# Third block's input linear by seven products of half size, with weight sums on GpSimd and rope angles in later slots

## The reference

```python
def third_block(x, c, positions, ...):
    h = rms_norm(x, g_pre) * (1 + scale) + shift
    proj = h @ w_in
    (q_lat, kv_lat, k_rope, z_mla, q_mb, k_mb, v_mb, z_mb, merge_logits) = split_cols(proj)
    q = rms_norm(q_lat, g_q_lat) @ w_uq             # with a rope part
    kv = rms_norm(kv_lat, g_kv_lat) @ w_ukv         # keys and values
    o_mla = causal_dense_attention(rope(q), [k, rope(k_rope)], v)
    y_mla = (o_mla * silu(z_mla)) @ w_o_mla
    o_mb = moba_attention(rope(q_mb), rope(k_mb), v_mb)
    y_mb = (o_mb * silu(z_mb)) @ w_o_moba
    g_a, g_b = split(sigmoid(merge_logits + b_merge))
    y = (g_a * y_mla + g_b * y_mb) @ w_out
    return x + gate * rms_norm(y, g_post)
```

## Time and profile before

| | us |
|---|---|
| median of three runs | 2348.59 |
| lowest, highest | 2347.05, 2350.40 |
| span of the profiled execution | 2347.6 |
| PE busy in it | 2237.0 (95%) |
| block 3, by PE's timeline | about 2080 to the end |

### The profile page before, as it was taken

One profiled execution on the slowest core, in us unless ns is written; L12 is line 12 of the kernel. 1 busy time (PEld: TensorE's weight loads), 2 busy tenths in 40 slices (PEclk: granted clock), 3 DMA queues, 4 the chain that ended last, 5 costly groups with the idle time before them and its releaser, 6 DMA issues. The chain is left out here.

```text
span 2347.6 us, 35478 instructions
## 1 busy us (share of the span) xinstructions
PE 2237.0 (95%) x14663; PEld 1529.2 (65%) x14663; DVE 912.5 (39%) x1950; ACT 421.2 (18%) x905; POOL 433.0 (18%) x363
## 2 busy tenths in 40 slices
PE   8999999999999998998999999999999999999997
PEld 7888899986799987877633333333333333368786
DVE  4242465645444655526323332222222222253322
ACT  2210220024111024124111111111111111123231
POOL 0110598720188850112000000000000000000000
PEclk9999999999999999999999999999999999999999
DMA  6334744465754444300999999999999999953322
GB/s 263 132 117 143 253 162 157 167 229 204 319 182 165 162 177 171 108 20 2 409 407 429 427 427 429 428 429 412 422 427 428 428 429 428 426 220 130 126 75 87
DMA packets 61009, 619.34 MB, mean 264 GB/s; under 512 B 6784, under 2 KB 8064, under 8 KB 12288
## 3 DMA queue, kind: packets, MB, share of 16 engines
q1 hardware_dynamic: 59184, 611.08, 65.0%
q10 hardware_dynamic: 1712, 6.63, 0.8%
HBM read 616.63 MB, written 1.05 MB: 263 GB/s over the span
## 5 line engine op out<-in xcount | busy, mean ns | idle before, releaser
L2966 PE MATMUL ps<-expert_ring,moe_xg 128*64 128x512 f32 x1280 | 282.1, 593 | 10.4 <-DMA expert_ring<-we_dram 10.2
L3005 PE MATMUL ps<-expert_ring,mix_y 128*64 128x512 f32 x1024 | 228.6, 596 | 10.4 <-DMA expert_ring<-we_dram 10.3
L2966 PEld LDWEIGHTS ps<-expert_ring,moe_xg 128*64 128x64 f32 x1280 | 90.4, 137 | 191.0 <-issue 166.9
L461 PE MATMUL ps<-x_res,ring 128*128 128x256 f32 x896 | 201.4, 383 | 8.7 <-DMA x_res<-x_dram 8.7
L461 PEld LDWEIGHTS ps<-x_res,ring 128*128 128x128 f32 x896 | 169.9, 192 | 33.2 <-DMA ring<-w_in_dram 8.6
L3254 DVE TENSOR_SCALAR mix_y<-ps 128x512 f32<-128x512 f32 x32 | 22.1, 691 | 414.8 <-PE ps L2966 414.8
L2785 POOL COPY unscaled_x<-modulations 128x8 f32<-128x8 f32 x1 | 0.2, 197 | 945.6 <-POOLq L3187 945.6
L2966 PE MATMUL ps<-ring,moe_xg 128*64 128x512 f32 x768 | 170.2, 598 | 0.2
L3005 PEld LDWEIGHTS ps<-expert_ring,mix_y 128*64 128x64 f32 x1024 | 69.9, 137 | 146.8 <-issue 127.6
L461 PE MATMUL ps<-third_h,ring 128*128 128x256 f32 x704 | 160.7, 384 | 1.0 <-DVE third_h L3748 1.0
L620 POOL TENSOR_TENSOR seven_weights<-ring 128x512 f32<-128x512 f32 (+1 forms) x72 | 94.1, 1307 | 326.0 <-DVE seven_x_turned L636 289.2
(11 more groups left out here) (607 smaller groups left out, 3365.1 us busy)
## 6 DMA issues: line engine op xcount, KB each, us to landing
expert_ring<-we_dram SPq DMA_DIRECT2D x144, 2048.0 KB, 23.3
ring<-we_dram SPq DMA_DIRECT2D x48, 2048.0 KB, 24.7
ring<-w_in_dram SPq DMA_DIRECT2D x55, 1024.0 KB, 4.9
ring<-ffn_up_dram SPq DMA_DIRECT2D x44, 1024.0 KB, 4.9
ring<-ada_dram SPq DMA_DIRECT2D x36, 1024.0 KB, 4.9
ring<-w_out_dram SPq DMA_DIRECT2D x16, 1024.0 KB, 5.0
ring<-ffn_dn_dram SPq DMA_DIRECT2D x16, 1024.0 KB, 4.9
ring<-ple_g_dram SPq DMA_DIRECT2D x8, 1024.0 KB, 6.1
```

The lines of the kernel that those rows point to most:

```text
L461: mm = pe.matmul(core.ps[:, bank_of[n, c], 0:TOK], w[:, k * PANEL + c * P:k * PANEL + c * P + P], sources[panel](k0 + k), start=(k0 + k == ...
L2966: mm = pe.matmul(ps[out, bank, :], xg[:, j % 4, j // 4, :], w[:, bank * D + at:bank * D + at + 512], start=False, stop=(j == 7))
L3005: mm = pe.matmul(ps[out, 2, :], hidt[:, at_k:at_k + S], w[:, i * D + at:i * D + at + 512], start=False, stop=(k == DT - 1))
```

## The change

Panels 3 to 19 of `w_in3` (17 panels, tiles 6 to 11, 16, 17, 22, 23, 28, 29, 34, 35, 40 to 59) are made by `SevenProducts`, numbered f0 to f16 here. Four things come with it. POOL makes four weight sums for each of them. DVE turns h at slot 0 (`turn_h`). On PE the even slot of such a panel stands behind the fourth of its seven products (`midway`), the odd slot at its end. The angles leave the block ahead of everything at slot 0 and go, a group each, to slots 7 to 10 of DVE; the sines go from slot 7 to 13 of ACT, the first rope from slot 8 to 14, the root of the latents' norm from slot 6 to 5. The copies of the roped key piece go from POOL to ACT, one behind each key tile's evacuation.

```diff
                         if product == 6:
                             mm.then_inc(core.first_done.sem, 1)
+                            if last and seven.midway:
+                                woven.advance()
                     mm.then_inc(core.panel_used.sem, 1)
                     if last:
                         woven.advance()
-                        woven.advance()
+                        if not seven.midway:
+                            woven.advance()
...
-    rope_slot = [8, 16, 16, 17, 17, 22, 22, 23, 23, 40, 41, 42, 43, 46, 47, 49, 50]
+    rope_slot = [14, 16, 16, 17, 17, 22, 22, 23, 23, 40, 41, 42, 43, 46, 47, 49, 50]
...
-        yield 6
+        yield 5
         wait(act, "lat_var", 1)
         act.activation(b3.lat_rs[:, :], b3.lat_rs[:, :], ACT.Sqrt).then_inc(*inc("lat_root"))
-        yield 7
+        yield 13
         wait(act, "angles_done", 1)
...
-        link(dve.tensor_copy(b3.pos[:, :], b3.pos_int[:, :]))
-        rope_angles(dve, link, core, b3)
-        dve.sem_inc(*inc("angles_done"))
         yield 5
         wait(dve, "lat_summed", 1)
...
-        yield 6
         wait(dve, "lat_root", 1)
...
-    def gpsimd(pool):
-
-        wait(pool, "roped", 1)
-        for t in range(DT):
-            pool.wait_ge(core.act_evac.sem, core.act_evac.at(b3.K0[t] + 1))
-            pool.tensor_copy(kv[64:96, t, :], lat[64:96, 3, :]).then_inc(*inc("keyed"))
-        yield
+    def angles(dve):
+        link = core.link("dve", dve)
+        yield 7
+        dve.wait_ge(core.const_loaded.sem, core.const_loaded.at(16))
+        link(dve.tensor_copy(b3.pos[:, :], b3.pos_int[:, :]))
+        for n, slot in enumerate((7, 8, 9, 10)):
+            yield slot
+            rope_angles(dve, link, core, b3, n)
+        dve.sem_inc(*inc("angles_done"))
...
+        def keys(ts):
+
+            def key(t):
+                which, take, _ = plain(kv, (t,))[0]
+
+                def after(e, link, wait_tile):
+                    wait_tile(e, b3.K0[t])
+                    wait(e, "roped", 1)
+                    e.activation(kv[64:96, t, :], lat[64:96, 3, :], ACT.Copy).then_inc(b3.sem["keyed"].sem, 1)
+                return (which, take, after)
+            return [key(t) for t in ts]
...
+        h_turned = s.enter_context(nc.sbuf_tensor("third_h_turned", [P, 4, DT // 2, P], F32))
...
+        seven = SevenProducts(core, s, {"w_in3": (3, turned_h, None, {0: 0})}, core.seven_signals, midway=True, prefix="third_seven_")
+
+        def turn_h(dve):
+            start.at(dve, "h_ready", DT)
+            seven.turn(dve, 0, h[:, 0:4, :], h[:, 4:8, :], *(h_turned[:, i, :, :] for i in (0, 2, 1, 3)))
+            yield
+        linear(core, sources, None, tiles, act_work=positions, banks=3, raw=start, seven=seven,
                weave=Weave((*pe_work, pe_att, outputs, pe_last), (start.shift, act_work, act_att, merge_biases, act_last),
-                           (dve_work, dve_att, dve_last), (pool_work,)))
+                           (turn_h, *dve_work, dve_att, dve_last)))
```

More of the change, by code:

```diff
@@ L563, with __init__ @@
     TURNED = {5: 1, 7: 2, 6: 3, 4: 4}
-    def __init__(self, core, s, parts, signals):
+    def __init__(self, core, s, parts, signals, midway=False, prefix="seven_"):
         def sb(name, shape):
-            return s.enter_context(core.nc.sbuf_tensor("seven_" + name, shape, F32))
-        self.core, self.names, self.groups = core, tuple(parts), {}
+            return s.enter_context(core.nc.sbuf_tensor(prefix + name, shape, F32))
+        self.core, self.names, self.groups, self.midway = core, tuple(parts), {}, midway
         self.first_pair, self.moving_of, self.keepers = {}, {}, {}
@@ L1797, in first_block @@
         parts_fast |= {name: (0, turned_h, keep, groups(name)) for name, keep in (("ffn_dn0", norms[1].keep), ("ffn_dn1", norms[3].keep))}
-        seven = SevenProducts(core, s, parts_fast, [core.counter("seven_" + n) for n in ("summed", "turned", "copied", "combined")])
+        core.seven_signals = [core.counter("seven_" + n) for n in ("summed", "turned", "copied", "combined")]
+        seven = SevenProducts(core, s, parts_fast, core.seven_signals)
         def turn_x(name, first, norm):
@@ L3763, in third_block @@
         b3.Q0, b3.MQ0, b3.MK0, b3.V0, b3.MV0, b3.K0 = 12, 4, 28, 30, 40, (24, 25, 26, 27, 36, 37, 38, 39)
-        pe_work, act_work, dve_work, pool_work, close = projections(core, b3)
+        pe_work, act_work, dve_work, close = projections(core, b3)
         def wait(eng, name, n):
@@ L3789, in third_block, with turned_h @@
                    ("w_om", lambda k: o[:, k, :]), ("w_ob", lambda k: o[:, 4 + k, :]), ("w_out3", lambda k: y[:, k, :])]
-        linear(core, sources, None, tiles, act_work=positions, banks=3, raw=start,
+        h_turned = s.enter_context(nc.sbuf_tensor("third_h_turned", [P, 4, DT // 2, P], F32))
+        def turned_h(product, k0, p):
+            return h_turned[:, {5: 0, 7: 1, 6: 2, 4: 3}[product], p, :]
+        seven = SevenProducts(core, s, {"w_in3": (3, turned_h, None, {0: 0})}, core.seven_signals, midway=True, prefix="third_seven_")
[4 more added lines that the diff above has]
+        linear(core, sources, None, tiles, act_work=positions, banks=3, raw=start, seven=seven,
                weave=Weave((*pe_work, pe_att, outputs, pe_last), (start.shift, act_work, act_att, merge_biases, act_last),
-                           (dve_work, dve_att, dve_last), (pool_work,)))
+                           (turn_h, *dve_work, dve_att, dve_last)))
         close()
```

30 lines of the change are left out of this document (14 added, 16 removed).

## The result

| us | before | after |
|---|---|---|
| median (lowest to highest) of 5 runs each | 2347.82 (2346.72 to 2350.40) | 2392.94 (2388.96 to 2394.91) |
| span of the profiled execution | 2347.6 | 2391.1 |

The changed kernel takes 1.0193 times as long (95% interval 1.0181 to 1.0204), +45.1 by the medians and +43.5 by the two spans. The sign of the forecast holds and its size (+29.6) doesn't: the time lies 2.9 above the range's upper end of 2390. Its main chain was met, and two terms were priced too low.

A forecast was written before the change was run, and what follows sets the result against it. TensorE's own stream, busy 95% of the span, was taken as the bound. Waits (a) to (d) 35.7, with (e) 40.7, less 11.1 saved by seven products, give +29.6, so 2378 us; range 2364 to 2390.

The forecast's parts named there:

- main chain: Fast panels: VectorE and ScalarE begin the even slot's work only after the whole panel is combined, so PE waits.
- the step held to be decisive: Even slot: PE reaches it in mid-panel, 3.57 after the start; VectorE goes on at panel's end +0.67, ScalarE at +0.79.
- (a): Slots 17, 23, 41, 43, 47: PE waits for VectorE's rope steps at a panel's end, 7.1 us in all.
- (b): Slots 35, 45, 47, 51, 53, 57, 59: PE waits for ScalarE's copies and scalings of the even slot, 12.0 us.
- (c): Mid-panel slots 41, 44, 50, 56: PE waits for chains begun only at the panel before's end, 9.2 us.
- (e): Tile 13: two angle groups on VectorE delay the third fast panel's combining; 5.0 us taken, 1.7 uncontended, 7.0 contended.
- What the sums cost: Fast panels: GpSimd's four sums take 5.27 us, below PE's 6.25, so the forecast costed them at nothing.
- the row at 837.00: Earlier trace: after a pause of 2.37 a product took 1.16, 0.1 lost; the forecast's model for waits of 2.
- Rival three: Block 3: the clock falls at each of a dozen waits of about 2 us, 2.0 each, giving 2402; chance 8%.
- (d): First scores, slot 28 to tile 33: PE waits 4.5, next panel 0.5 late, clock drop 2.4; 7.4 us.
- Rivals one and two: One: even slot's work is covered, 2337, 6%. Two: GpSimd's sums set the pace, no change, 2348.5, 4%.

The follow-up runs named there:

- the last versions: Changed kernel with the even slot in mid-panel on all three engines, seven products from panel 6 on, woven slots moved twice; the quoted range has median 2340.04.

## Why the prediction was right and wrong

**Right: the step held to be decisive.** (a) and (b) came out at 7.1 and 12.1 for 7.1 and 12.0, pause by pause. They rest on one chain, panel's end, combining, take, step, whose lengths stand in the earlier trace rows; and the run with the even slot in the middle took them away together with more than half of (c).

**The steps that failed.** The forecast put two things at nothing: what GpSimd's sums do to VectorE's chains, outside the angle groups, and the clock behind every pause but the one at tile 33.

**Right in kind, wrong in reach: contention.** Under (e) the forecast saw that an operation beside a GpSimd sum takes longer, took 5.0 between 1.7 and 7.0, and applied it to the angle groups behind the second panel alone. The trace has it in each place where a VectorE chain meets the sums. The first angle group, which the forecast left out, holds the second panel's combining 1.4 too long for the third. In (c) the ropes ahead of slots 41 and 44 lose 1.4 in two steps (2224.61: 1.38 for 0.42), and one softmax step ahead of 50 and 56 loses 0.8 (2262.69: 1.04 for a step of 128x4). Without the sums (c) is 8.0, so the forecast's 9.2 was 1.2 too much for the chains alone, and the sums add 4.5.

The wait at tile 13, 5.1 for a forecast of 5.0, was met by luck. The two groups that the forecast priced took 7.2 (2124.19 to 2131.4) for its 6.5, since GpSimd had no sums to make in most of that time and waited for weights; the rest came from the first group, at 7.8, which held up what stands behind it. Without the sums tile 13 waits 1.6, and the forecast's end without contention is 1.7. VectorE's and GpSimd's rows there:

```profile
2124.19 1.14 DVE L3516 TENSOR_SCALAR third_tab<-third_pos,mat 128x256 f32<-128x256 f32 x1
...
2131.47 0.29 DVE L650 TENSOR_TENSOR third_seven_second<-third_seven_part,ps 128x128 f32<-128x128 f32 x1
...
2132.11 1.27 POOL L623 TENSOR_TENSOR third_seven_weights<-ring 128x512 f32<-128x512 f32 x1 [6.93 <-DMA ring<-w_in_dram]
```

Under "What the sums cost" the forecast has "I cost it at nothing", and that was the failed sentence. It held for GpSimd's own pace and overlooked its neighbour's. The Trainium skill ("SBUF — State Buffer", section "SBUF: two separate sides") names both kinds of operations, those with two operands in SBUF and those in a two-port mode. The trace agrees for the two-operand kind (the subtractions, 4.20 for 1.34); one-operand steps lose as well (1.24 for 0.29), though no row tells which mode they run in. The forecast used this rule for (e) alone, and it bears on every chain beside the sums.

**Wrong: the clock.** The forecast paid 2.4 for one pause, at tile 33 (trace: 2.8), and nothing for the others, by the row at 837.00. Behind tile 13 it cost 3.1, behind slots 44, 56 and 57 4.8, and filling those pauses and the one at tile 33 gave 8.9 back (6.5 by the stretches). The pauses at 44 and 56 were longer than forecast (3.7 and 3.4 for 2.9 and 2.7), since contention had lengthened them, and so nearer to the one of 3.16 in the earlier trace rows than to those of 2.37. Without the sums, at 2.3 and 2.6, the clock stayed up behind 44 and fell behind 56. Length alone doesn't tell: the pause of 3.2 at slot 50 was followed by matmuls at full pace (2266.87). Rival three had this mechanism at twelve waits of 2.0; the changed kernel's trace shows it at four pauses, and at none of the 1.1 to 2.2 that stand by themselves, but with the pauses filled it came behind 1.90 and 1.76. What decides it beside the pause's length stays open. The 13.9 us between 29.6 and 43.5 are 4.6 in (e), 3.3 in (c), 1.1 in (d) and 4.8 outside the terms; all but the 1.1, most of which is small late starts, is clock and contention.

**Rivals one and two fell.** No new wait was covered, and GpSimd's four sums never ended a pause of PE: of PE's pauses over 0.15 us in block 3 none has GpSimd as its releaser.

**Open.** Runs of one kernel differ by up to 11 us in the last versions (2336.85 to 2347.61) with the mean granted clock between 0.997 and 0.991; the traces put several us of that ahead of block 3's products, and what makes it differ there wasn't tried.

## What to carry to other kernels

Work woven between a faster inner loop's pieces must move on *all* engines to the same piece; if the consumer's program still waits for the whole piece, a slot in its middle is worse than one at its end. Before spreading a sum over an idle engine, list what its neighbour on the memory does in the same microseconds, and price each of those steps. A saving of 0.65 a panel is smaller than one late handover of 1.1, so the slots have to fit before such a saving counts. And where the rest of a program varies by more than the change, compare the traces between two rows that both kernels share.

## What the hardware showed that was not expected

One-operand VectorE steps on data in SBUF (128x256, 0.29 alone) took 1.24 beside a GpSimd sum, one step for each sum, while GpSimd's rows there went from 1.27 to at most 1.46 (one in block 1 took 1.72). An angle group of 3.0 to 3.4 took 7.8 beside sums with gaps (2114.92 to 2122.7 in the changed kernel) and 11.5 beside sums without (2103.8 to 2115.2 in the run with the angles early). Steps that read PSUM kept their length in the midst of sums, and so did a reduction that reads and writes SBUF, 1.01 in the kernel before as well; VectorE's rows of the changed kernel beside the sums at 2259.96 to 2263.7:

```profile
2260.32 0.42 DVE L3635 TENSOR_TENSOR third_o<-ps,third_z 128x256 f32<-128x256 f32 x1
...
2260.66 0.95 DVE L3610 SCALAR_TENSOR_TENSOR third_prob<-ps,mat 128x768 f32<-128x768 f32 x1
...
2261.64 1.01 DVE L3616 TENSOR_REDUCE third_st<-third_prob 128x2 f32<-128x256 f32 x2
```

The step of 128x768 had 0.96 in the earlier trace rows, with no sum in the block. So it is not every step on SBUF that the sums hold up: the one-operand TENSOR_SCALAR steps cost as much as the two-operand ones, and the reduction cost nothing more.
